# Routing tables by one-hot matmuls, and expert rows gated and added to the residual in memory, in a diffusion layer with a 32-expert mixture

## The reference

```python
g_logits = xf @ wg + bg;  g_prob = softmax(g_logits);  g_sel = top_k(g_logits, 1)
e_in = e_logits[token, g_sel];  top_v, top_i = top_k(e_in, 2)
gate = softmax(top_v) * p_g
expert_id = g_sel * 8 + top_i
# the 4096 (token, expert) pairs are sorted by expert, each expert padded to
# blocks of 128 slots; per block, with e its expert:
yb = (silu(xblk @ w1[e]) * (xblk @ w3[e])) @ w2[e]
y[token] = sum over its two slots of gate * yb[slot]
x = layer_norm(ALPHA * x + g2 * y, ln2_g, ln2_b)
```

## Time and profile before

| What | Value |
|---|---|
| Three runs, us | 2516.97, 2518.12, 2529.49; median 2518.12 |
| Span of the profiled execution, us (no other time is given for it) | 2525.4 |
| Mean granted TensorE clock | 0.871 of full |
| Busy: PE, DVE, ACT, POOL | 1907.9, 1605.4, 987.0, 323.9 us (76, 64, 39, 13%) |
| Weight pieces of the experts | 186 of 1 MB, 11.0 us from issue to landing (median) |
| Store of a y block (ACT), us to landing | 6.2 (median of 50) |
| Stages | up to 1389; routing to 1475.7; experts to 2376.2; combine to 2525.4 |

### The profile page before, as it was taken

One profiled execution on the slowest core, in us unless ns is written; L12 is line 12 of the kernel. 1 busy time (PEld: TensorE's weight loads), 2 busy tenths in 40 slices (PEclk: granted clock), 3 DMA queues, 4 the chain that ended last, 5 costly groups with the idle time before them and its releaser, 6 DMA issues. The chain is left out here.

```text
span 2525.4 us, 42209 instructions
## 1 busy us (share of the span) xinstructions
PE 1907.9 (76%) x12030; PEld 1117.7 (44%) x12031; DVE 1605.4 (64%) x2156; ACT 987.0 (39%) x1260; POOL 323.9 (13%) x297
## 2 busy tenths in 40 slices
PE   6789999934317787869998039999999999999400
PEld 1167776712116666635555014554444444444100
DVE  1365454368867787766766643566678999745377
ACT  2032231255626666632221031444456767534111
POOL 0000000000002000011221320111111112101154
PEclk8989999966758898988888569999999999999755
DMA  9611010001032111023332272766688999949375
GB/s 352 208 39 63 33 52 31 26 29 36 36 144 73 45 40 40 31 90 123 117 115 92 61 226 77 263 249 240 232 321 318 400 398 399 338 151 351 139 252 200
DMA packets 169574, 405.95 MB, mean 161 GB/s; under 512 B 19348, under 2 KB 32052, under 8 KB 168500
## 3 DMA queue, kind: packets, MB, share of 16 engines
q1 hardware_dynamic: 146904, 326.69, 36.1%
q0 software_dynamic: 13120, 44.06, 5.2%
q10 hardware_dynamic: 9504, 34.61, 3.5%
HBM read 329.73 MB, written 75.60 MB: 160 GB/s over the span
## 5 line engine op out<-in xcount | busy, mean ns | idle before, releaser
L1779 PE MATMUL ps<-arena 128*128 x1200 | 456.8, 381 | 34.9 <-DVE arena L1699 33.8
L1699 DVE SCALAR_TENSOR_TENSOR arena<-arena 128x2048 f32 (+1 forms) x186 | 419.2, 2286 | 87.5 <-ACT arena L1632 45.5
L1780 PE MATMUL ps<-arena 128*128 x1200 | 456.3, 380 | 0.0
L1781 PE MATMUL ps<-arena 128*128 x1200 | 456.1, 380 | 0.0
L558 PE MATMUL ps<-arena 128*128 128x256 f16 (+1 forms) x2448 | 326.1, 296 | 21.5 <-DVE arena L469 21.5
L1626 ACT ACTIVATE arena<-arena 128x2048 f32 (+1 forms) x124 | 232.8, 1907 | 170.1 <-PEq L1378 65.6
L558 PEld LDWEIGHTS ps<-arena 128*128 128x128 f16 x2448 | 242.4, 100 | 99.6 <-issue 17.0
L1779 PEld LDWEIGHTS ps<-arena 128*128 128x128 f16 x1200 | 117.6, 98 | 177.5 <-issue 51.2
L1781 PEld LDWEIGHTS ps<-arena 128*128 128x128 f16 x1200 | 117.7, 98 | 138.2 <-issue 1.7
L1780 PEld LDWEIGHTS ps<-arena 128*128 128x128 f16 x1200 | 117.6, 98 | 130.0 <-issue 1.4
L921 PE MATMUL ps<-arena 128*128 (+1 forms) x768 | 103.8, 277 | 78.4 <-DMA arena<-qT_d 55.0
(11 more groups left out here) (247 smaller groups left out, 3003.9 us busy)
## 6 DMA issues: line engine op xcount, KB each, us to landing
arena<-w SPq DMA_DIRECT2D x186, 1024.0 KB, 11.0
y_d<-arena ACTq DMA_DIRECT2D x50, 512.0 KB, 6.2
arena<-w_mod SPq DMA_DIRECT2D x12, 2048.0 KB, 8.0
arena<-x SPq DMA_DIRECT2D x8, 1024.0 KB, 5.3
arena<-x SPq DMA_DIRECT2D x16, 512.0 KB, 4.4
x_d<-arena SPq DMA_DIRECT2D x16, 512.0 KB, 2.6
h_d<-arena SPq DMA_DIRECT2D x16, 512.0 KB, 2.9
arena<-x_d SPq DMA_DIRECT2D x16, 512.0 KB, 5.9
```

Of the source, the lines that this page charges most:

```text
L1699: return nc.vector.scalar_tensor_tensor(dst, src, scale, high, ALU.mult, ALU.subtract)
L1779: pe.matmul(out, high, part(buf, whi, at, 512), start=first, stop=False)
L1780: pe.matmul(out, high, part(buf, wlo, at, 512), start=False, stop=False)
L1781: return pe.matmul(out, low, part(buf, whi, at, 512), start=False, stop=last)
```

## The change

- Two zero tiles are stored behind row 2048 of `h2_d` and of `x1_d` in the first stage (instead of a small zero table); a slot that holds no token points at its own partition's row there. `slot_tok_d`, `y_d`, `slot_i`, `gates` and the zero stores go.
- Routing: top values by reductions and comparisons over all 16 tiles at once; counts in half precision, with a scan over tiles; the tables by matmuls. With `place[p, s, :]` the one-hot of a pair's position in its block and `block[p, s, :]` that of its block, the sum over 32 columns s of place^T x (block * token) gives the token of each slot, and the same with the gates, split into two half-precision parts, gives `gslot`, a gate for each slot.
- Experts: `scale_y` multiplies by the slot's gate as well, and GpSimd, between its gathers, adds the rows of `y0` to `x1_d` by an accumulating indirect transfer. `scale_y(n)` waits until that of n-1 has landed.
- Combine: reads `x1_d` alone, four buffers; ScalarE normalises; VectorE multiplies by the scale, GpSimd adds the bias in three of four tiles, VectorE in the fourth. Division by ALPHA is in the gates, and the epsilon is scaled to match.

```diff
@@ phase_modulation
-            sp.dma_start(g["slot_tok_d"].rearrange("(a b) o -> a (b o)", a=64), zi).then_inc(rows_st, 16)
+            for table in (g["h2_d"], g["x1_d"]):
+                sp.dma_start(table[SEQ:SEQ + P, :], spare).then_inc(rows_st, 16)
@@ phase_route, vector
-            for t in range(T):
-                link(V.max(v3("gm8", T, 8)[:, t, :], v3("pad8", T, 8)[:, t, :]))
-                link(V.max_index(v3("gi8", T, 8)[:, t, :].bitcast(U32), v3("gm8", T, 8)[:, t, :], v3("pad8", T, 8)[:, t, :]))
...
+            for k, top in enumerate(("m1", "m2")):
+                link(V.tensor_reduce(b[top], v3("elm", T, NE), AX_X, ALU.max))
+                link(V.tensor_tensor(v3("ea", T, NE), v3("elm", T, NE), spread(top, NE), ALU.is_equal))
+                first_of(b["ei"], "ea", "eb", NE)
+                link(V.tensor_tensor(by_expert(f"oh{k}"), io(NE).to_broadcast([P, T, NE]), spread("ei", NE), ALU.is_equal))
+                if k == 0:
+                    link(V.scalar_tensor_tensor(v3("elm", T, NE), by_expert("oh0"), 2 * NEG, v3("elm", T, NE), ALU.mult, ALU.add))
+            link(V.tensor_tensor(half("ohs16"), b["oh0"], b["oh1"], ALU.add))
+            dve.wait_ge(const, START + 6)
+            link(V.tensor_tensor_scan(b["cum"], b["first"], half("ohs16"), 0.0, ALU.mult, ALU.add))
...
+            link(V.tensor_tensor(h3("block", S), io(64).to_broadcast([P, S, 64]), spread("blkf", 64), ALU.is_equal))
+            link(V.tensor_tensor(h3("who", S), h3("block", S), spread("tokf", 64), ALU.mult))
+            link(V.tensor_tensor(h3("place", S), b["iotap"].rearrange("p (o n) -> p o n", o=1).to_broadcast([P, S, P]),
+                                 spread("posf", P), ALU.is_equal), "placed")
...
+            dve.wait_ge(mm, START + 3)
+            link(V.tensor_scalar(b["gaddr"], ps[:, 2, 0:64], 0.0, b["trash"], ALU.is_equal, ALU.mult))
+            link(V.scalar_tensor_tensor(gidx[:, 0:64], ps[:, 2, 0:64], -1.0, b["gaddr"], ALU.add, ALU.add))
...
+            dve.wait_ge(mm, START + 4)
+            link(V.tensor_scalar(gslot[:], ps[:, 3, 0:64], 1.0 / (GSCALE * W_SCALE * ALPHA), None, ALU.mult))
@@ phase_route, tensor
+            for s in range(S):
+                hit = pe.matmul(ps[:, 2, 0:64], h3("place", S)[:, s, :], h3("who", S)[:, s, :], start=(s == 0), stop=(s == S - 1))
+            hit.then_inc(mm, 1)
+            pe.wait_ge(gate_p, START + 12)
+            for s in range(S):
+                pe.matmul(ps[:, 3, 0:64], h3("place", S)[:, s, :], h3("gh", S)[:, s, :], start=(s == 0), stop=False)
+                hit = pe.matmul(ps[:, 3, 0:64], h3("place", S)[:, s, :], h3("gl", S)[:, s, :], start=False, stop=(s == S - 1))
@@ phase_route, gpsimd
-            for k in range(2):
-                for t in range(T):
-                    pool.indirect_dma_start(g["slot_tok_d"], bass.IndirectOffsetOnAxis(slot_i[:, k * T + t:k * T + t + 1], 0),
-                                            b["tok"][:, t:t + 1].bitcast(I32), None).then_inc(scat, 16)
-            pool.wait_ge(scat, 16 * 2 * T)
...
+            pool.wait_ge(v, START + mark["placed"])
+            G.tensor_tensor(h3("gh", S), h3("block", S), sp16("ghi16"), ALU.mult).then_inc(gate_p, 1)
+            G.tensor_tensor(h3("gl", S), h3("block", S), sp16("glo16"), ALU.mult).then_inc(gate_p, 1)
@@ phase_experts, gpsimd
-            with pool.Fori(0, (nb >> 1) + 1) as i:
+            def scatter(m):
+                pool.wait_ge(y_ev, START + m + 1)
+                pool.sem_inc(g["alone"], 1)
+                nc.gpsimd.tensor_copy(ix[:, 2:3], gidx[:, bass.ds(m, 1)]).then_inc(y_ix, 1)
+                pool.wait_ge(y_ix, START + m + 1)
+                pool.sem_inc(g["alone"], 1)
+                pool.indirect_dma_start(g["x1_d"], bass.IndirectOffsetOnAxis(ix[:, 2:3], 0), b["y0"], None, compute_op=ALU.add)\
+                    .then_inc(y_add, 16)
+            with pool.Fori(0, 2) as i:
                 gather(i, 0)
                 gather(i, 1)
+            with pool.Fori(2, (nb >> 1) + 1) as i:
+                gather(i, 0)
+                scatter(2 * i - 4)
+                gather(i, 1)
+                scatter(2 * i - 3)
+            with pool.Fori((nb >> 1) * 2 - 2, nb) as m:
+                scatter(m)
+            pool.wait_ge(y_add, nb * 16)
@@ phase_experts, scalar
-            def store_y(n):
-                act.wait_ge(y_ev, START + n + 1)
-                act.dma_start(g["y_d"][bass.ds(n * P, P), :], b["y0"]).then_inc(y_st, 16)
@@ phase_experts, vector
             def scale_y(n):
                 dve.wait_ge(y_mm, START + n + 1)
-                dve.wait_ge(y_st, START + 16 * n)
-                nc.vector.scalar_tensor_tensor(b["y0"], ps_row[:, 2560:3584], 1.0 / W_SCALE, b["g2"], ALU.mult, ALU.mult)\
+                if not isinstance(n, int) or n > 0:
+                    dve.wait_ge(y_add, 16 * n)
+                nc.vector.scalar_tensor_tensor(b["y0"], ps_row[:, 2560:3584], gslot[:, bass.ds(n, 1)], b["g2"], ALU.mult, ALU.mult)\
                     .then_inc(y_ev, 1)
@@ phase_combine, new
+    R = 4
+            def measure(t):
...
+            def shift(t):
+                j = t % R
+                dve.wait_ge(pw, START + t + 1)
+                nc.vector.tensor_scalar(b[f"shift{j}"], b[f"mv{j}"][:, 0:1], b[f"rs{j}"], -1.0, ALU.mult, ALU.mult).then_inc(shift_d, 1)
+            def scale(t):
+                j = t % R
+                dve.wait_ge(norm_a, START + t + 1)
+                if on_pool(t):
+                    nc.vector.tensor_tensor(b[f"o{j}"], b[f"o{j}"], b["l2g"], ALU.mult).then_inc(scaled, 1)
+                    return
...
+            measure(0)
+            for t in range(T_LAT):
+                if t + 1 < T_LAT:
+                    measure(t + 1)
+                shift(t)
+                if t:
+                    scale(t - 1)
```

More of the change, by code:

```diff
@@ L182, in phase_modulation @@
     c2a = small[:, 2 * KD:4 * KD]
-    zi = small[0:64, 128:256].bitcast(I32)
+    spare = arena[:, 3 * KD * 512 + 6 * D:3 * KD * 512 + 7 * D]
     wmod_v = g["w_mod"].rearrange("(k p) n -> p k n", p=P)
@@ L1365, in phase_route @@
     T = T_LAT
[L1366 to L1371, removed]
+    S = 2 * T
@@ L1510, in _ @@
[L1510 to L1514 removed]
+            G = nc.gpsimd
+            G.memset(half("ones16"), 1.0).then_inc(const, 1)
+            G.memset(b["first"], 1.0).then_inc(const, 1)
+            G.memset(b["one32"], 1.0).then_inc(const, 1)
@@ L1892, in _ @@
+            for t in range(T_LAT - 2, T_LAT):
+                if on_pool(t):
+                    move(t)
         @block.scalar
         def _(act):
-            def store(i, j):
-                act.wait_ge(v, START + NV * (2 * i + j + 1))
-                act.dma_start(g["out"][bass.ds((2 * i + j) * P, P), :], b[f"o{j}"]).then_inc(o_st[j], 16)
-            for j in range(2):
-                act.wait_ge(x_ld[j], START + 16)
-                nc.scalar.activation(b[f"xa{j}"], b[f"x1{j}"], ACT.Copy, scale=ALPHA).then_inc(a_x, 1)
@@ L1900, in _, with store @@
-            with act.Fori(0, LAST) as i:
-                for j in range(2):
-                    store(i, j)
-                    act.wait_ge(x_ld[j], START + 16 * i + 32)
-                    nc.scalar.activation(b[f"xa{j}"], b[f"x1{j}"], ACT.Copy, scale=ALPHA).then_inc(a_x, 1)
-            for j in range(2):
-                store(LAST, j)
-            for j in range(2):
-                act.wait_ge(o_st[j], START + 16 * (T_LAT // 2))
+            def store(t):
+                j = t % R
+                if on_pool(t):
+                    act.wait_ge(moved, START + t - t // 4 + 1)
+                else:
+                    act.wait_ge(scaled, START + t + 1)
+                act.dma_start(g["out"][t * P:(t + 1) * P, :], b[f"o{j}"]).then_inc(o_st[j], 16)
@@ new lines, in _ @@
+            for t in range(T_LAT):
+                j = t % R
+                act.wait_ge(shift_d, START + t + 1)
+                if t >= R:
+                    act.wait_ge(o_st[j], BEFORE + 16 * (t // R))
+                nc.scalar.activation(b[f"o{j}"], b[f"x{j}"], ACT.Identity, bias=b[f"shift{j}"], scale=b[f"rs{j}"]).then_inc(norm_a, 1)
+                if t >= 2:
+                    store(t - 2)
+            for t in range(T_LAT - 2, T_LAT):
+                store(t)
+            for j in range(R):
+                act.wait_ge(o_st[j], BEFORE + 16 * (T_LAT // R))
@@ L1940, in _constants @@
+            dve.wait_ge(ld, START + 32)
+            measure(0)
+            for t in range(T_LAT):
+                if t + 1 < T_LAT:
[3 more added lines that the diff above has]
+                    scale(t - 1)
+            scale(T_LAT - 1)
 def _constants():
```

315 lines of the change are left out of this document (153 added, 162 removed).

## The result

The changed kernel takes 2624.68 us (median of four runs, 2621.36 to 2630.35), beside 2520.4 us for the kernel before in the same set (2516.97 to 2529.49): ratio 1.041, 95% interval 1.038 to 1.043. It is slower, as forecast, and lies inside the range; but the forecast was 1% and 4.1% was measured.

A forecast was written before the change was run, and what follows sets the result against it. Experts: TensorE sets the pace where an expert has several blocks; elsewhere DMA is full and VectorE has little to spare. Routing -26, combine -63, experts +115 sum to +26: 2544 us from 2518.1, range 2470 to 2640.

The forecast's parts named there:

- T0: Experts: when TensorE has transposed the odd block of a pair, freeing gather A to start; dense `scale_y` forecast at 20.5 us after.
- six dense pairs, odd 25 to 35: Experts, every block a new expert: scatter waits stretch a pair from 36.85 to 45.1 us, +49 in sum.
- six mixed ones, 5, 9, 13, 19, 23, 43: Experts, block n+2 starts an expert: splits and `h_low` queue behind the stalled `scale_y`, 9 us late each, +54.
- 15, 17, 37, 39: Experts: blocks 15 and 17, with quick gathers, cost 4.5 us each, 37 and 39 together 9: +18.
- Light: nothing: Experts, light pairs: the delayed work is ready at 14.2 us, before TensorE wants it at 16.85, so no cost.
- start and end of the stage: Experts, end only: the last scatter, 9 us at most, replaces the last store: +4.
- emptier queues: Experts: stretched pairs leave the DMA queues emptier and gathers quicker, so 10 us are taken off.
- From it to the next T0 are 26.4 us of VectorE and TensorE work: Experts, dense pairs: work from the odd `scale_y` to the next T0 stays 26.4 us, less 1.8 of vanishing ScalarE waits.
- TensorE's clock still near 1.0: Sign that the forecast is right: TensorE's clock stays near 1.0.
- Rival A: Experts: the scatter lands 4.2 us from issue, like the quickest gathers; part +55, net -34, 2484 us; chance 0.33.
- B: Experts: the accumulate is dear, landing 15 us after issue; part +301, net +212, 2730 us; chance 0.12.
- C: GpSimd sets combine at 5.5 us a tile (-47) and routing yields 15: net +53, 2571 us; chance 0.14.

The follow-up runs named there:

- run 1: Changed kernel with GpSimd sending each scatter ahead of the gather instead of behind the gather's landing, one y buffer: 2450.95 us, ratio 0.971 to the kernel before.
- run 3: Changed kernel in its own issue order, but with two y buffers, one for odd and one for even blocks: 2446.89 us, ratio 0.970 to the kernel before.
- run 10: Changed kernel in its own order, one y buffer, with gather A's wait on TensorE's transposes one block less: 2450.9 us.
- run 2: Changed kernel with the add taken out of the scatter, so the output lacks the residual and one of two experts per token: 2584.61 us.
- run 7: Changed kernel with the scatters sent ahead of the gathers and the add taken out of the scatter, one y buffer: 2426.7 us.
- Runs 5 and 6: 5: VectorE's next table values read before the wait, against a pair-loop control (2615.27 us): 2592.81 us. 6: idle TensorE products added to the changed kernel: 2613.3 us.

## Why the prediction came out as it did

**Routing: the number right, -30 for -26, the end of the path wrong.** `placed` came within 1 us. Behind it two terms were too dear: 64 small matmuls were priced 0.227 us each from the earlier trace rows and stand 0.053 apart, 3.6 us instead of 14.5; the GpSimd products took 3.60 each where 4.7 stood. With TensorE done at 1437.5 the end was set by VectorE's block tables, which run until 1444.8 and which the prediction had called covered; it had named them as what stands next. They took back 7 of those 13 us, and so the sum came out near: that is luck.

**Combine: right in the main, -69 for -63.** The tile costs 3.6 us instead of 4.5, which alone would be -78; but the start and end of the stage, priced at 1, cost some 9: VectorE starts at 2556.5, 10.9 us into it, and after the last tile's first operation at 2610.1 there are 15.4 us to the end.

**Mechanism in the experts: right on which blocks wait and why.** The odd blocks wait (and one even one), and the cause is the order in GpSimd's program together with the single buffer: sending the scatter first (run 1), a second buffer (run 3) or a gather A that need not wait for T0 (run 10) each end the stall, and `scale_y` starts at T0 + 19.45 for 20.5. Landing and issue were each within 1 us in dense pairs. The Trainium skill, "Collectives: The Full Stack", section "The bandwidth ceiling", has an add need a second read; an estimate from it was 1.3 us a scatter. The runs agree that an add costs time, and of that size: 1.8 us in the median, and 375 against 398 GB/s where the queues are full. That it is a second read no run shows. The Trainium skill, "DMA: Bandwidth & Descriptors", section "Anatomy of one DMA", gave an estimate of 3.2 us for the transfer: a write without the add takes 3.3 at the quickest, which agrees, and 4.5 in the median of run 2 and 7.3 in that of run 7, with full queues, which does not. The one with the add takes 6.0 at the quickest.

**Sizes in the experts: wrong, +115 for +200.** The terms, from the starts of the even `scale_y` in both traces:

| Term of the prediction | forecast | measured |
|---|---|---|
| six dense pairs, odd 25 to 35 | +49 | +58.6 |
| six mixed ones, 5, 9, 13, 19, 23, 43 | +54 | +68.0 |
| 15, 17, 37, 39 | +18 | +31.6 |
| "Light: nothing": 7, 11, 21, 41, 45 | 0 | +31.1 |
| light: 1, 3, 47 | 0 | -0.3 |
| start and end of the stage | +4 | +11 |
| "emptier queues" | -10 | within the rows above |

Three steps failed.
- **"Light: nothing."** The largest miss. These pairs follow a long one and took 28.8 to 31.7 us, not 33.7: they caught up. The stall takes that away: this is an overlap that the prediction had wrong. The step also priced copy, gap and issue at 2.0, "VectorE being stalled", although in the pair shown VectorE was busy with splits (1710.63) and GpSimd needed 4.6.
- **"From it to the next T0 are 26.4 us of VectorE and TensorE work"**, less 1.8. It took 27.7 (2119.15 to 2146.85), 3.1 more than the sum had. The sum moved the work behind the wait unchanged; in fact VectorE's table reads, which cost next to nothing where it did not stall (7.9 us of bare issue in run 1, 55.1 in the change), came bare behind the wait (1.76 us), and TensorE started at its lower level (2.1 us). Laid beside the pair of the earlier trace rows, these 3.9 us are new and 2.6 us of waits are gone (VectorE on ScalarE 1.26, TensorE on a split 1.17, issue 0.2), which makes the 27.7 out of 26.4. The same holds in the other stalled pairs. In the six mixed ones `scale_y` starts at T0 + 18.5 to 20.1, forecast 18.7, but 27.0 to 28.5 us stand behind it, where the sum had some 24; at 15, 17 and 37 it starts 5 us later than before, forecast 4.5, and 2.3 to 3.9 more stand behind it. That accounts for the rows; by experiment it is not settled. Runs 5 and 6 took these two pieces on, and neither shortens the dense pairs by more than 2 us in twelve blocks.
- **"Minus 10 for emptier queues."** The emptier queues are there (gathers land in 5.5 us in the median, 7.3 before), but what they are worth is already in the row of T0 + 19.45, one microsecond a dense pair. And the end of the stage took 9.7 us more, against 4.

"TensorE's clock still near 1.0" was wrong for the same reason: it is 0.90. "None before even ones" was wrong by one wait of 3.5 us.

Rival A (landing at 4.2 from issue) fell: the quickest was 6.0. B (15 us after issue) fell too: the slowest was 11.5. C fell with combine at 3.6 us a tile. What no rival held is the stalled state's own price, in the rows 1.8 us of registers and 2 us of slow matmuls a stall.

**The whole in terms of runs:** stalls 174 us (change to run 1), the add's share of full queues 24 (run 1 to run 7), and 2426.7 then stands 98 below the 2524.3 of the kernel before in the same set, where routing and combine gave 99.

## What to carry to other kernels

Where one engine's program sends both loads and stores, write the store ahead of the load whose buffer comes free later: a store that is ready should not stand behind a wait for something younger. Price a stall as its length plus what comes bare behind it (register work, a clock that has to rise), and count it also in the short steps with which a pipeline catches up. Here, once the stall was gone, the add cost 19 us in the twelve dense blocks, where the queues were full (235.8 against 216.5), and 4 us in the 36 others; look at the DMA share of the stretch before you choose it.

## What was not expected of the hardware

- An accumulating indirect transfer of 128 rows keeps GpSimd 1.59 us, the plain one 0.99; it lands 6.0 us after issue at the quickest, the plain one 3.3.
- After 11 us without matmuls TensorE ran ten matmuls (4 us) at its lower level before it rose; after a gap of 2.94 us, behind 7.9 us of fp32 products, it still ran seven of them.
- A loop over pairs of blocks instead of single ones, with the same work, gave 9 us (2624.7 to 2615.3) in the stalled kernel; why is not shown.
- Matmuls of 64 columns in half precision start 0.053 us apart, at the 1.2 GHz level, a quarter of the 0.227 of the float32 ones of 36 columns in the earlier trace rows.
